# Gate and up products of three SwiGLU networks in the seven-product form

## The reference

```
x = x + 0.5 * swiglu(rmsnorm(x, ffn1_norm[i]), gate, up, down)   # networks f10, f11
x = x + mixer(rmsnorm(x, mix_norm[i]))      # pooling (i = 0), latent attention (i = 1)
x = x + 0.5 * swiglu(rmsnorm(x, ffn2_norm[i]), gate, up, down)   # networks f20, f21
swiglu(h, gate, up, down) = (silu(h @ gate) * (h @ up)) @ down
```

## Time and profile before

| what | value |
|---|---|
| median of 3 runs | 2552.53 us (2552.46 to 2553.2) |
| the profiled execution | span 2550.8 us from its first to its last instruction; the median lies 1.7 us above it |
| PE busy | 2514.7 us (99%), 11642 matmuls |
| DVE, ACT, POOL busy | 1215.6, 933.4, 622.4 us |
| chain that ended last | PE 89%, DVE 6%, ACT 2% |
| HBM | 88 GB/s over the span |

### The profile page before, as it was taken

The page is one execution under the profiler, slowest core; times in us unless marked ns, Lnnn a source line. Parts: engine busy times, 40 slices in busy tenths (PEclk is TensorE's granted clock), DMA queues, the critical chain, the costliest instruction groups (busy, mean ns, idle before and its releaser), DMA issues.

```text
span 2550.8 us, 28691 instructions
## 1 busy us (share of the span) xinstructions
PE 2514.7 (99%) x11642; PEld 2073.3 (81%) x11642; DVE 1215.6 (48%) x1607; ACT 933.4 (37%) x1371; POOL 622.4 (24%) x477
## 2 busy tenths in 40 slices
PE   8999999999999999999999999999999999999999
PEld 7777777888887888888888888888888888888887
DVE  5896655565635333335333333333336566433322
ACT  4486443444323332224333222332223554433221
POOL 3673403222203222101222101222101431322200
PEclk9999999999999999999999999999999999999999
DMA  5211312323232233332323332323332111333232
GB/s 171 71 46 58 105 44 67 107 92 98 93 99 81 90 93 98 98 97 75 107 92 96 96 99 88 108 93 97 92 100 87 42 50 58 94 96 95 93 99 93
DMA packets 66483, 227.26 MB, mean 89 GB/s; under 512 B 7216, under 2 KB 8752, under 8 KB 66352
## 3 DMA queue, kind: packets, MB, share of 16 engines
q1 hardware_dynamic: 66352, 225.44, 28.1%
HBM read 223.31 MB, written 2.10 MB: 88 GB/s over the span
## 4 chain that ended last, share of the span: by engine, by line
PE 89%; DVE 6%; ACT 2%; issue 1%; POOL 1%; DMA 0%; SPq 0%; DVEq 0%; ACTq 0%; POOLq 0%
PE main L386 19%; PE main L388 19%; PE main L387 19%; PE score L386 7%; PE score L388 6%; PE score L387 6%; PE out L386 3%; PE out L388 3%; PE out L387 3%; DVE wl L378 1%; DVE hxl L523 1%; DVE tmp L1347 1%; PE main L2055 1%; ACT wh L370 0%; PE turn L1027 0%
## 5 line engine op out<-in xcount | busy, mean ns | idle before, releaser
L378 DVE TENSOR_TENSOR wl<-raw,wh 128x1024 fp32r<-128x1024 f32 (+1 forms) x431 | 562.8, 1308 | 806.9 <-ACT wh L370 805.9
L370 ACT ACTIVATE wh<-raw 128x1024 fp32r<-128x1024 f32 (+1 forms) x431 | 439.9, 1024 | 635.7 <-PE main L388 473.2
L386 PE MATMUL main<-hxh,wh 128*128 128x512 f32 x1200 | 470.9, 392 | 8.2 <-DVE tmp L687 4.2
L388 PE MATMUL main<-hxh,wl 128*128 128x512 f32 x1200 | 467.9, 390 | 0.0
L387 PE MATMUL main<-hxl,wh 128*128 128x512 f32 x1200 | 467.8, 390 | 0.0
L386 PE MATMUL main<-hh,wh 128*128 128x512 f32 x880 | 342.4, 389 | 0.5 <-DVE wl L378 0.5
L387 PE MATMUL main<-hl,wh 128*128 128x512 f32 x880 | 342.3, 389 | 0.0
L388 PE MATMUL main<-hh,wl 128*128 128x512 f32 x880 | 342.3, 389 | 0.0
L452 POOL TENSOR_TENSOR acc<-acc,sq 128x512 f32<-128x512 f32 (+1 forms) x88 | 128.2, 1456 | 617.4 <-ACT sq L447 612.1
L386 PEld LDWEIGHTS main<-hxh,wh 128*128 128x128 f32 x1200 | 225.7, 188 | 60.1 <-DVE tmp L687 4.3
L388 PEld LDWEIGHTS main<-hxh,wl 128*128 128x128 f32 x1200 | 225.7, 188 | 47.5
(11 more groups left out here) (434 smaller groups left out, 3412.5 us busy)
## 6 DMA issues: line engine op xcount, KB each, us to landing
raw<-in_wts SPq DMA_DIRECT2D x375, 512.0 KB, 3.5
raw<-in_wts SPq DMA_DIRECT2D x52, 384.0 KB, 3.0
x<-in_xT SPq DMA_DIRECT2D x4, 512.0 KB, 8.3
out<-x SPq DMA_DIRECT2D x8, 256.0 KB, 3.2
memx<-in_memT SPq DMA_DIRECT2D x1, 1024.0 KB, 9.6
raw<-in_wts SPq DMA_DIRECT2D x4, 256.0 KB, 2.6
band<-in_pool SPq DMA_DIRECT2D x1, 768.0 KB, 4.2
rope<-in_rope SPq DMA_DIRECT2D x1, 512.0 KB, 7.1
```

The costliest lines, as they stand in the source:

```text
L370: e.activation(wh[i % NCONV][:, 0:n], raw[i % NRAW][:, 0:n], ACT.Copy).then_inc(*sig.up("weight_high", ("high", i)))
L378: e.tensor_tensor(wl[i % NCONV][:, 0:n], raw[i % NRAW][:, 0:n], f(wh[i % NCONV][:, 0:n]), ALU.subtract) \
L386: e.matmul(o, ah, bh, start=start, stop=False)
L388: return e.matmul(o, al, bh, start=False, stop=stop)
```

## The change

In f20, f11 and f21 the gate and up products of a tile are taken as one 2 x 2 block matrix (up and gate, each in a half of channels k 0 to 3 and one of k 4 to 7) by the 2 x 2 block matrix of the input (two halves of channels, two halves of 256 positions). The eight block products become seven, of sums of blocks. UP_LEFT, UP_RIGHT and GATE_RIGHT use the weights as they are, S1 to S4 use sums that POOL makes for each tile (`sum_step`). The input's sums `t1` and `t` are made once for a network (`block_split_scalar`, `block_split_vector`). A product is 4 blocks x 3 matmuls of 256 columns. The products of a tile share PSUM banks, and S2, S3 and GATE_RIGHT add on top of UP_LEFT's; ACT keeps copies between them (`keep_scalar`), and PE waits for those copies.

Weights are now handled in half-slots of 512 (6, and 8 in these networks; `raw` has 4 slots there), up to 6 half-slots ahead on ACT and DVE and up to 10 for the sums. `product_order` sets the order on all engines. The down product runs in three rounds, after tiles 0 to 7, 8 to 15 and 16 to 21; each round adds to x, by two instructions of DVE. rs is applied to gate, and to the down product, no longer to up. f10 and everything else compute as before.

```diff
+ROUNDS_OF = ((0, 8), (8, 8), (16, 6))
+BLOCKED = ("f20", "f11", "f21")
+UP_LEFT, UP_RIGHT, S4, GATE_RIGHT, S1, S2, S3 = 1, 2, 3, 4, 5, 6, 7
...
+def product_order(tiles, opening):
+
+    order = []
+    if opening:
+        order = [(0, UP_LEFT), (0, S1), (1, UP_LEFT), (1, S1)]
+        order += [(t, n) for n in (UP_RIGHT, S2, S3, GATE_RIGHT, S4) for t in (0, 1)]
+    first = 2 if opening else 0
+    for t in range(first, tiles):
+        order += [(t, UP_LEFT), (t, UP_RIGHT)]
+        if t > first:
+            order.append((t - 1, GATE_RIGHT))
+        order.append((t, S2))
+        if t > first:
+            order.append((t - 1, S4))
+        order += [(t, S1), (t, S3)]
+    return order + [(tiles - 1, GATE_RIGHT), (tiles - 1, S4)]
...
+            e.tensor_tensor(halves_of(wl, i), src, f(halves_of(wh, i)), ALU.subtract) \
+                .then_inc(*sig.up("weight_low", ("low", i), *([("free", ("sum", tile, which))] if which in (S1, S2, S3, S4) else [])))
...
+            if which == S1:
+                a, b, op = raw_half(r + 1, 0), raw_half(r + 1, 1), ALU.add
+            elif which == S2:
+                e.wait_ge(*sig.at(("summed", tile, S1)))
+                a, b, op = sums.of(("sum", tile, S1))[:, :], raw_half(r, 0), ALU.subtract
+            elif which == S3:
+                a, b, op = raw_half(r, 0), raw_half(r + 1, 0), ALU.subtract
+            else:
+                e.wait_ge(*sig.at(("summed", tile, S2)))
+                a, b, op = raw_half(r, 1), sums.of(("sum", tile, S2))[:, :], ALU.subtract
+            e.tensor_tensor(t[:, :], a, b, op).then_inc(*sig.up("weights_summed", ("summed", tile, which)))
...
+        def weights_ahead(step, e, i, halves=AHEAD):
+            for n in range(i + 1, reach(i, halves) + 1):
+                step(e, n)
...
+        def block_product(e, nm, c, which):
+            i = part_no[(nm, c), which]
+            h, lo = weights_of(i)
+            if which == UP_LEFT:
+                b, old = a_banks.take((nm, "a", c))
+                e.wait_ge(*sig.at(old))
+            elif which == S2:
+                b = a_banks.of((nm, "a", c))
+                e.wait_ge(*sig.at(("kept", nm, c, UP_LEFT)))
+            elif which == S3:
...
+                e.wait_ge(*sig.at(("kept", nm, c, S2)))
+            elif which == GATE_RIGHT:
+                b = a_banks.of((nm, "a", c))
+                e.wait_ge(*sig.at(("kept", nm, c, S3)))
...
+            e.wait_ge(*sig.at(("low", i)))
+            for k in range(4):
+                mh, ml, ready = moving(nm, which, k)
+                e.wait_ge(*sig.at(ready))
+                e.matmul(b[:, LEFT], h[:, k, :], mh, start=first and k == 0, stop=False, skip_group_check=not first)
+                e.matmul(b[:, LEFT], h[:, k, :], ml, start=False, stop=False, skip_group_check=not first)
+                made = e.matmul(b[:, LEFT], lo[:, k, :], mh, start=False, stop=k == 3, skip_group_check=not first)
+            made.then_inc(*sig.up("unit_done", ("unit", i)))
...
+                order = product_order(n, rnd == 0)
+                for s, (t, which) in enumerate(order[:-2]):
+                    block_product(e, nm, c0 + t, which)
+                    if rnd == 0 and s == 5:
+                        square_sums(e, nm, KC - 1)
+                    if rnd == 0 and s == 8:
+                        spread_rows(e, nm, ("root", nm))
+                for m in range(2):
+                    _, old = down_banks.take((nm, "bank", rnd, m))
+                    e.wait_ge(*sig.at(old))
+                    down_step(e, nm, rnd, m, range(0, 2))
+                    block_product(e, nm, c0 + n - 1, (GATE_RIGHT, S4)[m])
+                for m in range(2):
+                    down_step(e, nm, rnd, m, range(2, n - 1))
+                for m in range(2):
+                    down_step(e, nm, rnd, m, range(n - 1, n))
+                for m in range(2, KC):
+                    _, old = down_banks.take((nm, "bank", rnd, m))
+                    e.wait_ge(*sig.at(old))
+                    down_step(e, nm, rnd, m, range(n))
...
+        def gate_scaled_vector(e, nm, c):
+            t = tile_turn2.of((nm, "gate", c))
+            e.wait_ge(*sig.at(("rs", nm)))
+            e.wait_ge(*sig.at(("gate right", nm, c)))
+            e.tensor_tensor(t[:, RIGHT], t[:, RIGHT], rs[:, RIGHT], ALU.mult).then_inc(*sig.up("block_made"))
+            e.wait_ge(*sig.at(("unit", part_no[(nm, c), GATE_RIGHT])))
+            e.tensor_tensor(t[:, LEFT], a_banks.of((nm, "a", c))[:, LEFT], rs[:, LEFT], ALU.mult) \
+                .then_inc(*sig.up("block_made", ("gate", nm, c), ("free", (nm, "a", c))))
...
+                order = product_order(n, rnd == 0)
+                for s in range(len(order) + 2):
+                    if s < len(order):
+                        t, which = order[s]
+                        weights_ahead(high, e, part_no[(nm, c0 + t), which])
+                        if which in (UP_LEFT, S2, S3):
+                            keep_scalar(e, nm, c0 + t, which)
+                    if rnd == 0 and s == 9:
+                        keep_rows(e, nm)
+                    if 1 <= s <= len(order) and order[s - 1][1] == GATE_RIGHT:
+                        silu_scalar(e, nm, c0 + order[s - 1][0])
+                    if s >= 2 and order[s - 2][1] == S4:
+                        t = order[s - 2][0]
+                        h_high_scalar(e, nm, c0 + t, t, ended)
...
+                for s, (t, which) in enumerate(product_order(n, rnd == 0)):
+                    weights_ahead(low, e, part_no[(nm, c0 + t), which])
+                    if rnd == 0 and s == 6:
+                        mean_square(e, nm, 1.0 / D)
+                    if which == UP_RIGHT:
+                        up_left_vector(e, nm, c0 + t)
+                    elif which == S3:
+                        gate_right_vector(e, nm, c0 + t)
+                    elif which == GATE_RIGHT:
+                        gate_scaled_vector(e, nm, c0 + t)
+                    elif which == S4:
+                        up_right_vector(e, nm, c0 + t)
+                for m in range(KC):
+                    weights_ahead(low, e, down_unit(nm, rnd, m), 4)
+                    y, old = tile_turn2.take((nm, "y", rnd, m))
+                    e.wait_ge(*sig.at(old))
+                    e.wait_ge(*sig.at(("unit", down_unit(nm, rnd, m))))
+                    e.scalar_tensor_tensor(y[:, :], down_banks.of((nm, "bank", rnd, m))[:, :], 0.5, rs[:, :], ALU.mult, ALU.mult) \
+                        .then_inc(*sig.up("y_scaled", ("y", nm, rnd, m), ("free", (nm, "bank", rnd, m)), *([("free", ("rs", nm))] if (rnd, m) == (2, KC - 1) else [])))
+                    e.wait_ge(*sig.at(("y", nm, rnd, m)))
+                    e.tensor_tensor(x[:, m, :], x[:, m, :], y[:, :], ALU.add) \
+                        .then_inc(*sig.up("x_even", ("x", nm, m) if rnd == 2 else ("x", nm, rnd, m), ("free", (nm, "y", rnd, m))))
+                    if rnd == 2 and next_nm in BLOCKED:
+                        block_split_vector(e, next_nm, m, next_gain, ("x", nm, m))
+                    elif rnd == 2 and next_nm:
+                        split_low(e, next_nm, m, next_gain)
...
+                order = product_order(n, rnd == 0)
+                for s in range(len(order) + 3):
+                    if s < len(order):
+                        t, which = order[s]
+                        weights_ahead(sum_weights, e, part_no[(nm, c0 + t), which], AHEAD + 4)
+                    if rnd == 0 and s == 6:
+                        inverse_root(e, nm)
+                    if 1 <= s <= len(order) and order[s - 1][1] == S4:
+                        join_gpsimd(e, nm, c0 + order[s - 1][0])
+                    if s >= 3 and order[s - 3][1] == S4:
+                        t = order[s - 3][0]
+                        h_low_gpsimd(e, nm, c0 + t, t)
...
+            if m < 4:
+                e.activation(hxh[:, m, LEFT], x[:, m, LEFT], ACT.Copy, scale=g).then_inc(*sig.up("x_high", ("b1 high", nm, m)))
+                e.activation(tsum[:, m, 0:Q], x[:, m, RIGHT], ACT.Copy, scale=g).then_inc(*sig.up("x_high", ("x right", nm, m)))
+                e.wait_ge(*sig.at(("t1 sum", nm, m)))
+                e.activation(hxh[:, m, RIGHT], t1sum[:, m, RIGHT], ACT.Copy, scale=g).then_inc(*sig.up("x_high", ("t1 high", nm, m)))
+                square(e, nm, m, x[:, m, :])
+            else:
+                e.activation(hxh[:, m, :], x[:, m, :], ACT.Copy, scale=g).then_inc(*sig.up("x_high", ("b2 high", nm, m - 4)))
+                square(e, nm, m, x[:, m, :])
+                block_turned_scalar(e, nm, m - 4)
...
+            e.activation(th[:, k, :], tsum[:, k, :], ACT.Copy).then_inc(*sig.up("x_high", ("t high", nm, k)))
...
+            if m < 4:
+                e.tensor_tensor(t1sum[:, m, RIGHT], x[:, m, RIGHT], x[:, m, LEFT], ALU.subtract).then_inc(*sig.up("x_low", ("t1 sum", nm, m)))
+                e.wait_ge(*sig.at(("b1 high", nm, m)))
```

(26 more changed lines are left out.)

336 lines of the change are left out of this document (287 added, 49 removed).

## The result

Four executions of the changed kernel have a median of 2661.9 us (2658.4 to 2664.8), beside 2552.5 for the kernel before: ratio 1.043, 95% interval [1.041, 1.044]. It is slower, as forecast, but by 109 us where 16.5 were forecast, and outside the range.

What follows compares the result with a forecast made beforehand. PE's work was taken as the limit, the other engines having room. Terms: 2550.8 - 55.8 + 29 + 37 + 6 = 2567 us of span, or 2569 us as median of the runs; range 2516 to 2612.

Steps and rivals of the forecast that it cites:

- Term 1: PE's gate and up products: 84 matmuls of 256 columns a tile replace 48 of 512, at 0.1195 us each; -55.8 us.
- restarts PE: Rival on PE's products: each product's waits make a break and the next matmul starts slowly; 2615 us, chance 0.03.
- The figure of the Trainium skill: Matmul start-to-start as N/2.4 plus about 2.5 ns; would make the saving on PE -78 us and the sum 2547.
- Term 2: Port of DVE and POOL in the tiles: they hold each other up, 11.0 us a tile over PE's 10.04; +29 us.
- Packs badly: Rival on the port of DVE and POOL: 11.8 us a tile, costing 70 us; 2610 us, chance 0.12.
- Whole operations exclude each other: Rival on the port: DVE and POOL operations never overlap, 13.0 us a tile, +131 us; 2670 us, chance 0.03.
- Term 3: Entries of the three networks: longer input splits on DVE and ACT make PE wait, mainly at UP_RIGHT; +37 us.
- Term 4: The rest: one more DVE operation behind the last matmul, and slow clock after long waits; +6 us.
- the buffers hold: Rival: look-ahead absorbs the port's excess (0 to 5 us) and entries cost 22; 2520 us, up to 2545, chance 0.34.
- what I said would show it: Signs: matmul step near 0.12 us, tile period 11, `kept` or `wl` releasing PE, longer low parts, 13 to 15 us idle at UP_RIGHT.

Runs made afterwards that it cites:

- raw5: The changed kernel with five raw slots of weights in the three networks in place of four; 2632.8 us.
- earlyx: The changed kernel with DVE updating x in the last groups before it splits groups 4 and up for f20 and f21; 2658.7 us.
- warm: The changed kernel with 16 matmuls of 256 columns on constants ahead of the second product (S1 of tile 0) of each network; 2661.2 us.
- psumlow3: The changed kernel with the first operand of 512-wide low parts of product weights read from PSUM from tile 3 on (wrong numbers); 2592.5 us.
- late8: The changed kernel with raw5, earlyx, POOL's inverse root ahead of its step's sums, and rounds of 6, 8, 8 tiles in place of 8, 8, 6; 2613.0 us.
- psumlow: The changed kernel with the first operand of 512-wide low parts of product weights read from PSUM in rounds two and three (wrong numbers); 2613.1 us.

## Why the prediction was wrong

- **Term 1 held.** The median step between matmuls of 256 columns, nearly all of them in the products, is 0.120 us over 6073 steps; 0.1195 was forecast. -55.8 stands, and no product restarts PE. The figure of the Trainium skill (page TensorE: Matmul & The Clock Gate, section "Wait — 56ns, not 53.3ns?"), which I weighed there, would have made it too good.
- **Term 2 is the step that failed**, 92 us against 29, in the mechanism that it named. Per network the sums cost 13.5 to 14.9 us in round one, 9.3 in round two and 5.2 to 7.0 in round three (6.5, 2.6, 0.6 forecast). Three things were mis-sized. The time of a tile on the port: 11.45 us by raw5, where I took 11.0. What is paid: the slack was about right, since four tiles pass unnoticed, but every tile behind them costs PE 1.4 us, and the last one 2.9, where I let the last 1.4 tiles off. And the raw slots, which I took for granted: with four of them POOL waits for fetches that late low parts hold up, 29 us over the kernel; raw5 shows it, and even with five the sums cost some 63. Two rivals stand near. "Packs badly" (2610) had a tile at 11.8, but term 2 alone exceeds its 70. "Whole operations exclude each other" (2670) comes nearest to 2661.9, by luck: its tile of 13.0 us is refuted by raw5's 11.45 for the same operations, its term 2 is 131 against 92, and term 4 fills the gap.
- **Term 3 was right in sum, not in detail**: the new splits cost 32 to 35 us, 37 forecast. The long wait was not at UP_RIGHT but at S1, for a PSUM bank; earlyx shows that this place doesn't matter, since DVE's work ends when it does.
- **Term 4 is the other step that failed**: 41 us against 6, with sums and splits taken away. I looked at f11's entry for the splits alone and missed the loop of DVE and ACT in the last down round, which needs 4.84 us even with the plain split (0.69 of it for the second operation on x, 1.46 for a `low` of 768 beside POOL's squares), against PE's 4.08. Without the second operation the time falls by 13 us; the rest of the 41 is read from PE's rows and not tested by a run of its own. I forecast nothing for the step from f11 to the mixer, which has it too. I also missed that the opening takes six PSUM banks, the last ones freed by DVE; before, and the earlier trace rows showed an entry without such a wait. The slow clock takes some 38 us of PE's steps in the changed kernel, 11 in the one before, though warm shows that part of it only fills a wait.
- **The rival "the buffers hold" (0.34)** rested on an average over a round. The average was irrelevant: a down product, where the port is nearly idle, makes up only for the next four tiles.
- Of what I said would show it, two did: `kept` releases S2, and low parts take 1.08 us (of sums) and 1.28 (of raw weights) on the average. The idle time that I put at UP_RIGHT stood at S1.

What stays open: how the 92 us divide between port and raw slots in round one (psumlow3 leaves tiles 0 to 2 out), how much of the last down round another order of ACT would give back, and whether a mixture of old and new tiles, which would bring the port under PE's time, beats the kernel before; it wasn't tried. None of the versions that leave nothing out does: the best, late8, has a ratio of 1.024 to before, [1.023, 1.026]. With sums and splits left out (nosum_oldsplit) it is 0.995, [0.993, 0.997].

## What to carry to other kernels

Before moving work from PE to POOL and DVE, add up, for each tile, the time in which one of them holds up the other, and treat anything near PE's time as over it: here 69% of the time by DVE's own durations became 93%, and PE paid for each tile beyond the queues' slack. Then look at the places where one stage hands over to the next, group by group, with every operation that the change adds, every PSUM bank that the next stage wants, and every loop in which two in-order engines wait for each other in turn: such a loop can be longer than the work of either. A wait that moves when the order is changed, at the same cost, points to an engine that is full, if its busy share (97 to 100% here) says so too.

## What the runs showed of the hardware

- An operation of DVE with two SBUF inputs beside a busy POOL takes 1.1 to 1.3 us on the average at 512 columns, up to 1.8, and 1.4 at 256; with one operand in PSUM it takes 0.685 at 512. POOL's operations stretch too: `sum<-raw,sum` takes 1.67 us on the average in the changed kernel, 1.47 in psumlow.
- A matmul with its own weight load takes 0.120 us from start to start at 256 columns and 0.2267 at 512, 53% for half the columns.
